# One-element operations of the next function, ahead of ScalarE's waits, in a two-block model kernel

## The reference, cut to what matters

```python
def rms_norm(x, g):
    xf = x.astype(jnp.float32)
    y = xf * lax.rsqrt(jnp.mean(xf * xf, axis=-1, keepdims=True) + EPS)
    return (y * g.astype(jnp.float32)).astype(x.dtype)

def hgrn2_mix(h, g_norm, w_in, g_out, w_out, lb):      # 16 heads of 128
    u = rms_norm(h, g_norm) @ w_in                     # q, f, i, z of each head
    q = jax.nn.silu(q).astype(jnp.float32)
    fg = lb + (1.0 - lb) * jax.nn.sigmoid(f.astype(jnp.float32))
    logf = jnp.log(fg)
    k = 1.0 - fg
    b = jnp.cumsum(logf, axis=3)                       # in chunks of 64 tokens
    q_intra = q * jnp.exp(b - b_mid)
    k_intra = k * jnp.exp(b_mid - b)
    ...
    o = rms_norm(o, g_out.reshape(HG_HEADS, HG_VDIM)).reshape(bsz, L, D_MODEL)
    return (o * jax.nn.silu(z)) @ w_out

# fox_shared_kv: k = rms_norm(k, g_k), and a log-sigmoid of 16 forget columns
# fox_mix:       q = rms_norm(q, g_q), softmax of the logits, silu(z)
```

## Time and profile before

| | us |
|---|---|
| Median of 3 runs | 3206.25 (3204.25 to 3206.61) |
| Profiled execution, its own time | 3205.97 |
| Profiled execution, span | 3204.1 |
| TensorE matmul busy | 3089.6 (96%) |
| VectorE busy | 1885.6 (59%) |
| ScalarE busy | 1637.4 (51%) |
| GpSimd busy | 673.5 (21%) |
| Mean granted TensorE clock | 0.976 |

### The profile page before, as it was taken

The page is one execution under the profiler, slowest core; times in us unless marked ns, Lnnn a source line. Parts: engine busy times, 40 slices in busy tenths (PEclk is TensorE's granted clock), DMA queues, the critical chain, the costliest instruction groups (busy, mean ns, idle before and its releaser), DMA issues.

```text
span 3204.1 us, 64061 instructions
## 1 busy us (share of the span) xinstructions
PE 3089.6 (96%) x25426; PEld 3003.3 (94%) x25426; DVE 1885.6 (59%) x3340; ACT 1637.4 (51%) x2621; POOL 673.5 (21%) x291
## 2 busy tenths in 40 slices
PE   8999998999999999877999999999999999999998
PEld 8999998999999898756999999999999999999998
DVE  5545555654444458666677788744447865554444
ACT  5666665566677642375444443444444444444443
POOL 3333332444434333202444410000000000000000
PEclk9999998999999899987999999999999999999999
DMA  5434343444433354312455544455554455555554
GB/s 194 142 134 141 136 141 107 171 171 170 145 132 137 112 180 154 118 66 106 162 180 184 183 146 146 172 179 188 184 183 171 156 175 184 183 184 183 183 185 156
DMA packets 72288, 506.60 MB, mean 158 GB/s; under 512 B 7904, under 2 KB 10592, under 8 KB 11232
## 3 DMA queue, kind: packets, MB, share of 16 engines
q1 hardware_dynamic: 71584, 503.09, 45.4%
q10 hardware_dynamic: 576, 1.72, 0.1%
HBM read 502.69 MB, written 2.10 MB: 158 GB/s over the span
## 4 chain that ended last, share of the span: by engine, by line
PE 89%; DVE 6%; ACT 2%; issue 2%; DMA 0%; DVEq 0%; SPq 0%; ACTq 0%
PE bank L439 14%; PE bank L440 14%; PE bank L441 14%; PE bank L2099 8%; PE bank L2097 8%; PE bank L2098 7%; PE bank L1890 5%; PE bank L1891 5%; PE bank L1892 5%; PE bank L452 3%; PE bank L1879 1%; DVE c_acc L1233 1%; PE bank L684 1%; DVE wlo L423 1%; DVE e_col L1982 1%
## 5 line engine op out<-in xcount | busy, mean ns | idle before, releaser
L416 ACT ACTIVATE whi<-raw 128x1024 fp32r<-128x1024 f32 x898 | 940.8, 1057 | 1039.2 <-PE bank L441 527.2
L423 DVE TENSOR_TENSOR wlo<-raw,whi 128x1024 fp32r<-128x1024 f32 x668 | 812.9, 1228 | 469.3 <-ACT whi L416 468.4
L423 POOL TENSOR_TENSOR wlo<-raw,whi 128x1024 fp32r<-128x1024 f32 x230 | 612.9, 2665 | 1092.0 <-ACT whi L416 1086.5
L439 PE MATMUL bank<-xa_hi,whi 128*128 128x272 f32 (+1 forms) x2064 | 605.6, 293 | 5.2 <-DVE xa_lo L1465 3.0
L440 PE MATMUL bank<-xa_lo,whi 128*128 128x272 f32 (+1 forms) x2064 | 597.4, 289 | 0.0
L441 PE MATMUL bank<-xa_hi,wlo 128*128 128x272 f32 (+1 forms) x2064 | 596.8, 289 | 0.0
L2099 PE MATMUL bank<-e_coef_hi,wlo 128*128 128x256 f32 x2048 | 575.3, 281 | 0.0
L2097 PE MATMUL bank<-e_coef_hi,whi 128*128 128x256 f32 x2048 | 574.5, 281 | 0.0
L2098 PE MATMUL bank<-e_coef_lo,whi 128*128 128x256 f32 x2048 | 569.9, 278 | 0.0
L439 PE MATMUL bank<-xb_hi,whi 128*128 128x256 f32 (+1 forms) x1536 | 440.3, 287 | 8.6 <-DVE f_qg L982 6.1
L440 PE MATMUL bank<-xb_lo,whi 128*128 128x256 f32 (+1 forms) x1536 | 436.8, 284 | 0.0
(11 more groups left out here) (388 smaller groups left out, 4491.5 us busy)
## 6 DMA issues: line engine op xcount, KB each, us to landing
raw<-in_w SPq DMA_DIRECT2D x251, 1024.0 KB, 4.8
raw<-in_v SPq DMA_DIRECT2D x128, 1024.0 KB, 5.3
raw<-in_u SPq DMA_DIRECT2D x96, 1024.0 KB, 4.8
hT<-in_hT SPq DMA_DIRECT2D x4, 544.0 KB, 8.3
out<-hT SPq DMA_DIRECT2D x8, 256.0 KB, 2.7
r_keys<-in_keys ACTq DMA_DIRECT2D x1, 1024.0 KB, 4.9
c_mask<-in_masks ACTq DMA_DIRECT2D x1, 320.0 KB, 3.0
params<-in_params SPq DMA_DIRECT2D x1, 238.5 KB, 2.7
```

The lines of the kernel that those rows point to most:

```text
L416: act.activation(whi[:, (2 * t.q + half) % 4, :], raw[:, t.q, half * 1024:(half + 1) * 1024], ACT.Copy).then_inc(w_hi_done, 1)
L423: eng.tensor_tensor(wlo[:, t.q, at], raw[:, t.q, at], whi[:, slot, :].bitcast(F32), ALU.subtract).then_inc(w_lo_done[half], 1)
L439: te.matmul(ps, hi, x[0][:, kk, cols], start=(kk == 0), stop=False)
```

## The change

A helper `table_for(act, function)` issues one ScalarE operation on one element: it reads the constant `one`, applies the given function, and writes one of eight new columns of `token` in turn. It is called seven times in the program text, each time directly ahead of a `wait_ge`, with the function of the operation behind that wait: the square root at the end of `out_scalar`; Sigmoid, Ln, Exp and Ln in `hgrn_scalar`; Ln in `kv_scalar`; Ln in `qz_scalar`. In HGRN, keys and values, and queries and gates each call is executed once for each of 16 heads, in `out_scalar` once per use, three times. `token` grows from 24 to 32 columns, and what is allocated behind it moves by as much. No wait, semaphore, DMA or operation of another engine is touched.

```diff
-        token = tensor(ctx, "token", [P, 24])
+        token = tensor(ctx, "token", [P, 32])
...
+        tables_asked = [0]
+
+        def table_for(act, function):
+
+            tables_asked[0] = (tables_asked[0] + 1) % 8
+            k = 24 + tables_asked[0]
+            act.activation(token[:, k:k + 1], con("one"), function)
...
             ch.run(body, 1, 3, 2)
+            table_for(act, ACT.Sqrt)
             act.wait_ge(sum_done, SUM_BEFORE[base] + 1)
             act.activation(root[:, 0:n], SUM[:, 0:n], ACT.Sqrt, bias=con("eps"), scale=1.0 / D)\
...
                 if within(p, HEADS):
+                    table_for(act, ACT.Sigmoid)
                     act.wait_ge(evacuated, 4 * p + 4)
...
+                    table_for(act, ACT.Ln)
                     act.wait_ge(fg_done, h)
...
+                    table_for(act, ACT.Exp)
                     act.wait_ge(cum_done, h)
...
+                    table_for(act, ACT.Ln)
                     act.wait_ge(osum_done, h - 1)
...
+                        table_for(act, ACT.Ln)
                         act.wait_ge(ksum_done, h)
...
+                        table_for(act, ACT.Ln)
                         act.wait_ge(qsum_done, h)
```

## The result

| | us |
|---|---|
| Kernel before, median of the runs beside it | 3206.58 (3204.25 to 3209.74, 6 runs) |
| Changed kernel, median | 3229.72 (3227.65 to 3234.00, 6 runs) |
| Ratio | 1.0075, 95% interval 1.0065 to 1.0085 |
| Profiled execution after: its own time, span | 3228.26, 3226.3 |

A forecast was written before the change was run, and what follows sets the result against it. TensorE, busy 96% of the span, was taken as the bound. Gain 0, additions +0.35 us in HGRN's drain and +0.1 in the queries' drain, about +0.5 in all: 3206.7 us, range 3203.3 to 3211, no change.

The forecast's parts named there:

- What bounds the kernel: Whole kernel: TensorE, busy 96% of the span; ScalarE edits count only where TensorE waits for it, in the drains.
- No load leaves a wait's shadow: All seven changed places: table loads (1283 ns) already start before the wait, so the change gains 0.
- Rivals 1 and 2: Drain loads leave waits, 3199.9 us, 2 in 100; additions bring loads, 3251 us, 3 in 100 including a dearer-addition form.
- rival 2's milder form: HGRN's filled passes and the drains: one addition costs 0.43 us, giving 3213.6 us; 3 in 100 together with added loads.
- The price of one addition, 0.1 us, and the covers: ScalarE: each addition delays its next operation 0.1 us; in filled passes 0.90 us of slack before L662 hides three.
- The shift of later tiles by eight columns ... cost 0, with no row against it: Tiles behind `token`: moving them changes no size or order of any transfer or operation, so cost 0.
- The clock (rival 3): HGRN's filled part: nine more long heads from TensorE's clock, 3220 us, 2 in 100; lucky draw, 3199, 1 in 100.

The follow-up runs named there:

- e2_ops: Changed kernel with all 99 added operations but `token` left at 24 columns, so every tile lies where it lay before: 3207.68 us, ratio 1.0002.
- e1_room: Kernel before with only `token` grown from 24 to 32 columns, no operation added: 3230.42 us, ratio 1.0075.
- e10_raw: Kernel before with 8 unused columns between `sq2` and `raw`: 3209.93 us, ratio 1.0010.
- e9_room40_alone: Kernel before with only `token` grown to 40 columns, no operation added: 3200.40 us, ratio 0.9979.
- e11_ops8: e2_ops with eight one-element operations instead of one for each call in `hgrn_scalar`: 3220.61 us, ratio 1.0047.
- e6_all64: e1_room with 8 more unused columns ahead of `rinv`: 3226.67 us, ratio 1.0064.
- e7_all32: Kernel before with 8 unused columns ahead of `rinv`, so every tile but two of constants lies 32 bytes higher: 3210.21 us, ratio 1.0013.
- e4_whi: Kernel before with `token` at 32 columns and 8 unused columns between `whi` and `hT`: 3214.66 us, ratio 1.0033.

## Why the prediction was wrong

**What bounds the kernel:** right in that TensorE does. But from "busy 394.26 of 395 us" the prediction went to "nothing waits there", and from that to nothing that can change. A busy TensorE can still be faster or slower: its time for one matmul is a term of its own, 3089.6 us over 25426 matmuls, and 1% of that is 31 us, more than both waits of the earlier trace rows together (10.1 us).

**No load leaves a wait's shadow:** right at all seven places, by the loads' count and by the row at 522.05; e2_ops, 1.0002, measures the gain and the cost together as nothing. Rivals 1 and 2 are out: no load went and none came, and one addition costs 0.10 us, not the 0.43 of rival 2's milder form.

**The price of one addition, 0.1 us, and the covers:** right. 203 ns each and 0.10 us to the next operation's start (523.35 to 523.45). The real operation behind it is shorter by some 0.02 (L752: 487 ns, now 470). From the load's start to the real operation it is 1.40 us (522.05 to 523.45), as forecast. The cover went from 0.90 to 0.82 us, and the drain from L731 to L753's end from 509.25 + 0.43 - 498.43 = 11.25 us to 511.85 + 0.43 - 500.73 = 11.55: +0.30, forecast +0.35. ScalarE's idle time ahead of L416 did not fall by 10 us, it rose from 1039.2 to 1049.3, since TensorE, which it waits for, had become slower: the first sign in the groups that the loss was TensorE's. With the tiles in place (e2_ops) it fell, to 1031.8, by 7.4.

**"The shift of later tiles by eight columns ... cost 0, with no row against it":** this is the step that failed, and alone it is the whole miss: forecast 0, measured 22.9 us with nothing else changed (e1_room, 3230.42 against 3207.49). There was indeed no row for it, and that was the error: where the prediction had no row for one addition, it bounded it from both sides (0 to 0.43 us); a shift of most operands of the engine that bounds the kernel got neither a bound nor a rival, and each per cent of 3089 us is 31. The gaps between matmuls were in the trace, uneven from one to the next (112 to 123 ns from start to start in the part by v, without a wait) and repeating every twelve matmuls: a pattern that equal work on equal shapes does not explain. That it hangs on place was not to be read from it; e10_raw and the changed kernel, with other patterns, show it.

**The clock (rival 3):** a small part at most, and within what the forecast allowed (five long heads, give or take two). Of the fourteen intervals between heads in the filled part six are long now, where five were; one long head is 1.5 us. One of the six, from the chain (start, us, what; the columns of the earlier trace rows):

```profile
257.90 0.84 PE bank L708 x8
289.10 0.84 PE bank L708 x8
```

Half of the loss lies in the v stretch, at a granted clock of 1.00 in both kernels.

The fastest placement of those tried is `token` at 40 columns, 3200.40 us with no added operation (ratio 0.9979, interval 0.9970 to 0.9989) and 3194.41 with them (0.9951, 0.9934 to 0.9967). The gain of e9_room40_alone does not lie in the v stretch as a whole, which takes 2.0 us more than before (1117.3); part u is faster there (1708), and the v stretch begins at 2075.0 us instead of 2079.8. The two versions with 40 columns differ in part 2 of the profiled executions (1690 and 1722 matmuls in the same 200 us) with all tiles in the same places, at a clock of 1.00 in both; they ran on two chips, and one has the added operations. Why the pace there has more than one value in one placement is open, and it limits what is said above: distance does not fix the pace in every case.

Open as well is the mechanism under the distance: whether the load of the next weights and the read of the moving operand of one matmul get in each other's way, or TensorE and the writes of other engines. For TensorE alone speaks that the counts repeat to one or two matmuls in kernels whose other engines run differently (in part u, VectorE has 151 operations in the kernel before and 161 in e11_ops8, and TensorE 1693 and 1692 matmuls); it was not tested apart.

## What to carry to other kernels

A change that allocates even a few columns in front of the operands of the bounding engine is two changes; time it once with the memory alone and once with the work alone. When a fully busy engine's busy time changes at an equal count of instructions, look at its time per instruction in a stretch without waits, at a clock of 1.00, before looking at any wait. And before moving work into a wait, see whether it isn't there already: here the table load stood in front of the waiting operation from the start.

## What the runs showed of the hardware

- TensorE's pace changed with how far apart its operands lie in a partition, by steps as small as 32 bytes: 117.7 to 119.9 ns per matmul (300 us over 2549 and 2503) for the same 128x128 by 256 columns in fp32, at a granted clock of 1.00. Between placements alone the kernel before ranged from 3200.40 us (e9_room40_alone) to 3230.42 (e1_room). No start modulo 64 bytes explains it: all starts at multiples of 64 bytes (e6_all64) was one of the slow placements. One placement showed two paces in part 2: 118.3 and 116.1 ns (200 us over 1690 and 1722).
- A table load (1283 ns) is followed by its operation 1.30 us after its start (498.84 to 500.14), and it starts right behind ScalarE's previous operation, before the semaphore for which its operation waits (load at 519.45, the awaited sum done at 520.76, the operation at 520.80).
- How often the clock falls in the first block differs from kernel to kernel: granted 0.97 to 1.00 in 90 to 485 us, with 3060 matmuls (e7_all32) and 3151 (e4_whi) in the same time.
